# Issue order of the row gathers on GpSimd: two slots' u rows, then two slots' v rows

## The reference, cut to what matters

```python
u_sel = jnp.take(u, expert, axis=0)
v_sel = jnp.take(v, expert, axis=0)
act = jax.nn.gelu(jnp.einsum('btd,bthkd->bthk', hx, u_sel), approximate=False)
return jnp.einsum('bthk,bthkd->btd', (gate * act), v_sel)
```

## Time and profile before

| what | value |
|---|---|
| median of 3 runs | 2037.94 us (2035.21 to 2042.11) |
| the profiled execution | 2036.36 us, with a span of 2034.6 us |
| TensorE busy | 1774.8 us (87%) |
| VectorE busy | 1356.7 us (67%) |
| GpSimd busy | 1037.5 us (51%) |
| ScalarE busy | 854.1 us (42%) |
| chain that ended last | PE 41%, DMA 31%, POOL 10%, DVE 8% |

### The profile page before, as it was taken

How to read it: one execution, slowest core, us unless ns; L and a number is a source line. 1 busy time by engine, 2 the same in 40 slices (tenths; PEclk the granted TensorE clock), 3 DMA queues, 4 the chain that set the end, 5 groups by cost and what they waited for, 6 DMA issues and landing times.

```text
span 2034.6 us, 21815 instructions
## 1 busy us (share of the span) xinstructions
PE 1774.8 (87%) x6507; PEld 1006.1 (49%) x6507; DVE 1356.7 (67%) x2955; ACT 854.1 (42%) x2034; POOL 1037.5 (51%) x1064
## 2 busy tenths in 40 slices
PE   8999777779988897797898977977777999999998
PEld 6655222213344452243545424422222897778997
DVE  4577988556478569846975994454554367578874
ACT  3444434330157133313742444343433455655663
POOL 0767777765567657755775676667775000000000
PEclk9999999999999899998998998999999999999999
DMA  7999999999999999999999999999999554455664
GB/s 282 388 407 408 409 409 409 409 402 388 378 406 383 408 409 409 409 409 400 379 403 409 409 409 409 409 409 406 409 409 388 180 180 139 130 161 175 187 188 136
DMA packets 194308, 704.27 MB, mean 346 GB/s; under 512 B 21624, under 2 KB 23040, under 8 KB 193936
## 3 DMA queue, kind: packets, MB, share of 16 engines
q0 software_dynamic: 152064, 553.72, 68.9%
q1 hardware_dynamic: 40672, 147.44, 21.0%
q10 hardware_dynamic: 1456, 1.72, 0.2%
HBM read 701.60 MB, written 1.06 MB: 345 GB/s over the span
## 4 chain that ended last, share of the span: by engine, by line
PE 41%; DMA 31%; POOL 10%; DVE 8%; issue 6%; ACT 3%; SPq 0%; DVEq 0%; ACTq 0%; POOLq 0%
DMA a<-in_peer_v,eidx 17%; PE ps L967 17%; DMA a<-in_peer_u,eidx 13%; PE ps L678 11%; POOL a L507 5%; POOL a L519 5%; PE ps L584 5%; DVE a L2022 3%; PE ps L701 3%; PE ps L830 2%; DVE ring_r L2209 1%; PE ps L713 1%; PE ps L637 0%; ACT a_r L1608 0%; DVE a L2163 0%
## 5 line engine op out<-in xcount | busy, mean ns | idle before, releaser
L678 PE MATMUL ps<-a,diag 128*128 128x512 f32 (+1 forms) x1880 | 906.1, 614 | 210.5 <-DMA a<-in_peer_v,eidx 165.3
L2022 DVE SCALAR_TENSOR_TENSOR a<-a,ps 128x1024 f32<-128x1024 f32 x528 | 641.3, 1219 | 397.0 <-DMA a<-in_peer_u,eidx 373.2
L678 PEld LDWEIGHTS ps<-a,diag 128*128 128x128 f32 (+1 forms) x1880 | 329.5, 189 | 734.6 <-issue 647.7
L507 POOL DMA_INDIRECT a<-in_peer_u,eidx x528 | 518.0, 981 | 317.2 <-DVE a L2022 155.1
L519 POOL DMA_INDIRECT a<-in_peer_v,eidx x528 | 518.6, 982 | 211.5 <-issue 132.7
L1348 ACT ACTIVATE gel<-dots 128x1 f32<-128x1 f32 x528 | 104.3, 201 | 697.2 <-DVE a L2022 692.0
L967 PE MATMUL ps<-a_r 128*128 128x256 f32 (+1 forms) x1096 | 258.9, 327 | 0.4 <-DVE a_r L2268 0.4
L967 PEld LDWEIGHTS ps<-a_r 128*128 128x128 f32 x1096 | 181.9, 188 | 21.7 <-issue 2.8
L2209 DVE TENSOR_TENSOR ring_r<-wring,a_r 128x1024 fp32r<-128x1024 f32 x95 | 116.0, 1223 | 82.0 <-ACT a_r L1608 81.6
L1360 ACT ACTIVATE diag<-cstc,cga 128x128 f32<-128x128 f32 (+1 forms) x398 | 158.3, 398 | 13.1
L967 PE MATMUL ps<-a_r,ring_r 128*128 128x256 f32 x512 | 142.5, 278 | 0.0
(11 more groups left out here) (301 smaller groups left out, 1783.7 us busy)
## 6 DMA issues: line engine op xcount, KB each, us to landing
wring<-in_units SPq DMA_DIRECT2D x246, 512.0 KB, 4.5
a<-in_peer_u,eidx POOLq DMA_INDIRECT x528, 13.0
a<-in_peer_v,eidx POOLq DMA_INDIRECT x528, 13.1
late<-in_units SPq DMA_DIRECT2D x8, 512.0 KB, 15.6
a<-in_units SPq DMA_DIRECT2D x7, 512.0 KB, 14.7
a<-in_poolm SPq DMA_DIRECT2D x1, 1632.0 KB, 8.5
late<-in_cs SPq DMA_DIRECT2D x1, 1280.0 KB, 8.0
h<-in_xin SPq DMA_DIRECT2D x2, 512.0 KB, 4.3
```

The source lines that it names most:

```text
L507: g.indirect_dma_start(ug[:, n % NU, :], None, peer_u, bass.IndirectOffsetOnAxis(ap=eidx[:, t, k:k + 1], axis=0))\
L678: last = nc.tensor.matmul(ps[0:P, b + j, :], diag[:, pe_slots[n] % ND, 0:P], vg[:, k % NV, j * 512:(j + 1) * 512], start=False, stop=n == ...
L2022: v.scalar_tensor_tensor(ug[:, n % NU, :], ug[:, n % NU, :], 1.0, ps2(0) if t == 2 else ps2(4), ALU.mult, ALU.mult, accum_out=dots[:, k % ...
```

## The change

GpSimd's loop advances by two slots. In each turn it issues the u gathers of slots k and k + 1, and then the v gathers of slots k - 2 and k - 1. Before, each turn had the u gather of slot k and the v gather of slot k - 2. Waits, buffers, counts and all other engines' programs are the same.

```diff
-                    for k in range(count + V_BEHIND):
+                    for k in range(0, count + V_BEHIND, 2):
                         if k % 16 == 0 and (l, t, k // 16) in [p[0:3] for p in PICKS]:
                             g.wait_ge(S("eidx"), tk_number(l, t, k // 16))
                         if k < count:
-                            row_u(t, k, base + k)
+                            for m in (k, k + 1):
+                                row_u(t, m, base + m)
                         if k >= V_BEHIND:
-                            row_v(t, k - V_BEHIND, base + k - V_BEHIND)
+                            for m in (k - V_BEHIND, k - V_BEHIND + 1):
+                                row_v(t, m, base + m)
```

## The result

The changed kernel takes 2043.68 us (median of 20 runs, 2040.53 to 2046.56); the kernel before, timed with it, 2039.59 us. The ratio is 1.0020, with a 95% interval of 1.0014 to 1.0027: 4.1 us slower. That is inside the predicted range and under the 0.3% that the prediction took as the edge of what can be told, but twenty runs of each tell it clearly: where no change was forecast there is a small, real loss. (One of the twenty runs of the kernel before took 2945.67 us, in a slower state that a few executions fall into; the ratio leaves it out.)

The account below looks back on a forecast made before the run. The gather part was taken as DMA-bound at 409 GB/s, followed by a dense part with TensorE busy. Terms: 2036.36 - 1.3 + 1.3 = 2036.4 us profiled, 2037.9 us as a median, no change; range 2028 to 2049 us.

Parts of the forecast that it names:

- The bound, the ceiling and the bookkeeping: Gather part, to about 1577 us: DMA-bound, ceiling 409 GB/s; four stretches below it lose 16.3 us, all that reordering could win.
- VectorE's 58 sums: VectorE's own sums: v rows land 1.28 us later, at most 74 us idle, covered by u-row waits; 0, ends 0 and +24.
- The rival that priced it: Attention stretches: 19 VectorE sums wait 1.28 us each, 24 us, 2062 us; with a third of them 8 us; chance 0.12.
- The prediction's own signs of being wrong: Among them: gather part over more than 6 us sooner or later; lower rate from 600 to 660 or 960 to 1040 us.
- A u ahead of a blocked v: 470 to 560 us: one more u queued before GpSimd waits for TensorE's v buffer; -1.3 us, ends 0 and 5.3 gained.
- a v behind a blocked u: Where the queue runs dry, as 440 to 470 us: v stands behind a u waiting for a dot; +1.3 us at most.
- Bursts cool TensorE: 660 to 960 us: longer gaps between v pairs lower TensorE's clock, 14 us, 2052 us if nothing covers it; chance 0.04.
- Coefficient: v(n) six gathers behind u(n) instead of five: GELU and coefficient get 1.28 us more, buying nothing at a full queue; 0.
- GpSimd beside VectorE: Attention stretches: issues lengthened by VectorE make GpSimd the bound; order changes only which issues; 0, ends plus and minus 8.9 us.
- The threshold: Whole kernel: a measurement tells apart about 0.3%, 6 us; no change had 0.73, slower 0.16, faster 0.11.

Follow-up runs that it names:

- early sums: The kernel before, gathers in the old order, with VectorE's own sum of slot n one dot earlier, behind dot(n+1): 2051.20 us, 1.0054.
- v before u: The kernel before, still one gather of each in turn, but v(k-2) issued ahead of u(k): 2045.19 us, 1.0022; on another chip 0.9971.
- late sums: VectorE's own sums one dot later, behind dot(n+3): in the changed kernel 2041.76 us, 1.0011; in the kernel before 2041.55 us, 1.0004.
- without own sums: The kernel before with VectorE's 58 slots given to TensorE: 2057.03 us with gathers in turn, 2056.91 us in pairs, both 1.0083.

## Why the prediction was wrong

**The bound, the ceiling and the bookkeeping** held. In each trace of an even chip the DMA time lost from 440 to 1560 us goes with the span. Against the 16.3 us of the kernel before, the loss is 8.9 us more for the change, 18 for early sums, 11 for v before u, 5.5 and 5.0 for the late sums (with pairs and in the old order), 22 and 23 without own sums, counted in the same way; the spans are 8.4, 16.1, 8.3, 5.4, 5.2, 21.0 and 21.3 us longer.

**VectorE's 58 sums, "Term: 0",** is the step that failed. The mechanism was described rightly, one gather later against the dot, for even and odd slots alike, with the wait moving from the dots (373 to 318 us) to the sums (16 to 65 us, 49 more where 74 was the most). What was wrong is the cover. The 373 us of waits for u rows are a sum over all 528 slots; I set them against 58 places without asking whether such a wait stands behind each of them. At 447 us none does: the norm's chain follows. The price of one wait was off as well: 27 of the 58 sums waited, 2.4 us each and up to 4.8 us where weights share the DMA engines, not 1.28 us each. The change as a whole costs 4.1 us by the medians; that this is the size of this term rests on the pair of kernels without own sums, where the loss is 0. How much of it is the wait of the sums, and how much such meetings of issue and sum or the order of the gathers around a late dot, stays open. The rival that priced it named only the attention stretches and 8 to 24 us; the trace shows it at the start of the projections (440 to 600 us), and smaller. That rival, with a chance of 0.12, named the likely cause, the wrong size and the wrong place: from 600 to 660 us, where it put eight sums, the rate did not change (383 GB/s), and from 600 to 660 and 960 to 1040 us together the sums waited only 2 us. The prediction's own signs of being wrong were met: the last v rows land over 6 us later in the trace, and the rate is lower from 960 to 1040 us.

**A u ahead of a blocked v, -1.3, and a v behind a blocked u, +1.3.** Neither is seen alone. The gain did not come: 470 to 560 us went from 385 to 380 GB/s. The cost comes behind a late dot, as at 456.65 us, so it can't be parted from the term above; without own sums both together are 0 (2056.91 against 2057.03 us).

**Bursts cool TensorE.** The clock from 660 to 960 us did fall from 0.95 to 0.93, and the gaps in front of v rows are longer, but the rate there is 409 and no time is lost. From 440 to 470 us the clock fell from 0.89 to 0.77, and it did so in the kernel with early sums too (0.77), whose gathers come in turn. The kernels without own sums have the same bursts and no loss. As a cause it has nothing for it in these traces.

**Coefficient and GpSimd beside VectorE,** 0 each. Over the whole kernel that held: the mean gather issue went from 0.981 and 0.982 to 0.979 and 0.974 us, so the order did not make issues meet VectorE more often: 33 issues were lengthened by a sum of VectorE, where before it was 39. In one place it did not hold: from 440 to 470 us a meeting that before just missed cost 1.0 us. That GpSimd is the bound in the first attention stretch has something for it: without own sums the mean issue there is 0.96 us instead of 1.06, and the rate 403 GB/s instead of 383.

**The threshold.** The text took 6 us as what can be told. With 20 runs of each the interval is 1.3 us to either side, so a sum of two guesses of 1.3 us and one of 0 should have been weighed as a small loss or gain, not as none. Of the terms put at 0 only the one that made VectorE wait had its ends on one side alone (0 and +24 us).

## What to carry to other kernels

When an edit moves a transfer later against an in-order consumer, look up each place where the consumer takes it, and what stands behind that place in the consumer's program; a large total of other waits covers it only where such a wait comes next. And price such a wait by the gather's time in that stretch, not by its time at a queue that nothing shares. In a stretch that is DMA-bound throughout, multiply each dip below the ceiling by its length: that sum moved with the span to within some 3 us in these traces, and it shows in which stage a change pays. A cheap test of such a theory is to move the consumer instead of the transfer: early sums with no gather moved made a loss three times as large. It shows that such waits can cost, not that they are all that the change cost.

## What the runs showed of the hardware that was not expected

**An issue beside a sum of VectorE.** In the trace of before 39 gathers began to be issued 0.1 to 1.1 us behind the start of one of VectorE's own sums (1.28 us long). However late they began, they ended 2.09 to 2.11 us behind that start, so they took 0.98 to 1.99 us in place of 0.94. One that began up to 0.09 us behind the start, or ahead of it, took 0.94 us. The changed kernel has 33 such issues with the same ends. The sum beside the issue at 458.05 us is:

```profile
457.89 1.28 DVE L2045 SCALAR_TENSOR_TENSOR acc<-a,cgt,acc 128x1024 f32<-128x1024 f32 x1
```

It ends at 459.17, the issue at 459.98. Before, the issue at 456.52 us began 0.01 us behind a sum and took 0.93 us. In all this took 23 us of GpSimd's time before and 21 us after.

**Two kinds of chip.** The kernel before took 2035 to 2045 us on some chips and 2130 to 2175 us on others, about 5% apart; in the traces of its variants on the latter the DMA rate of the gather part is mostly between 340 and 400 GB/s in place of 409. Each chip was seen on one occasion, so whether it is the chip or what went on beside it at the time is not shown. An order of issue that lost 0.2% on an even chip (v before u, 1.0022) gained 0.3% on an uneven one (0.9971, 0.9951 to 0.9990). So an order tuned on one such chip need not be the best on the next, and effects of this size should be compared on the same one.
